# The front of a hybrid decoder layer: unrolled steps, raw x transposed early, its norm applied at the projection reads

## The chip, the cores and the metric

One NeuronCore of a Trainium2 chip runs the whole layer. The metric is the device time of one execution in microseconds (us). Smaller is better.

## The reference, cut to what matters

```python
u    = rms_norm(x, mix_norm_w)                       # x: 1024 tokens x 1024
proj = u @ w_in                                      # columns b, c, h (512 each), q (512), k and v (128 each)
y_conv = b * causal_dwconv3(c * h)                   # three taps over the tokens
q, k = rms_norm per head of 64
y_attn = sliding_window_attention(q, k, v, sinks)    # 8 heads on 2 key heads, blocks of 128, window 128, ALiBi
x = x + concat(rms_norm(y_conv), rms_norm(y_attn)) @ w_out
xn = rms_norm(x, ffn_norm_w)
x = x + moe_ffn(xn, ...)   # 64 experts, top 8 of them per token, and one shared expert
```

All of it is float32, but for a few small counting matmuls.

## The kernel before, in words

The kernel has two parts. The front works through the tokens in 8 tiles of 128 and does everything up to the router. The routed part then runs the shared expert and some 80 jobs of expert rows.

A semaphore orders every pair of instructions of different engines that depend on each other. Each engine's program is written out by hand and is run strictly in that order; a wait holds up all that is behind it on that engine. In the front each engine has a function `step`. Step T works on three tiles: N, the next one (its projections), T itself (its attention and its output projection), and B, the one before (its router).

PE runs in step T, in this order: `scores(T)`, `t_x(N)` (transposes of the normed x of the next tile), `project(N, 0)` and `project(N, 1)` (groups c and h), `t_xn(B)`, `t_p(T)`, `project(N, 2)` (b), `p_v(T)`, `router(B)`, `project(N, 3)` (q), `t_y(T)`, `project(N, 4)` (k and v), `position(B)`, `out_project(T, 0)`, `t_qk(N)`, `out_project(T, 1)`. A projection group of 512 columns is 8 matmuls of 128x128 by 512, each of which the trace shows as two instructions. `project` writes to two banks psP in turn, and ACT copies each out (`read_group`).

What lies around the first group: x has two tiles `x_sb`. The sum x1 of `x1_add(T)` (DVE, after `out_project(T, 1)`) goes to a tile of its own, and frees the x tile for SP's `load_x`. ACT squares the loaded x (`x_square`), DVE and POOL make the factor of the norm (`x_rms`, L476), ACT writes x times that factor to `xs` (`x_scale`, L909), PE transposes it, DVE reads the transposes into `uT` (`read_uT`, L1124), and `project(N, 0)` can start. The tile `xs` is also that of `xn`, the normed x1.

DVE in step T: `x_rms(N)`, `read_uT(N)`, `soft_a(T)`, `soft_b(T)` (scale, bias and maximum of the scores), `xn_make(B)`, `u_mul(N)` (c times h), `o_norm(T)`, `y_rms(T)`, `route(B)`, `read_yT(T)`, `read_pos(B)`, `qk_norm(N)`, `conv(N)`, `slots(B)`, `x1_add(T)`. The taps of the convolution need the product c*h moved by one and two tokens: SP stores it to DRAM and loads it twice, shifted (`shift_u`).

ACT in step T: `x_square(N)`, `x_scale(N)`, `exps(T)`, groups 0 and 1 of N, `read_xn(B)`, `read_p(T)`, group 2, `sigmoid(B)`, `y_square(T)`, `y_scale(T)` (both halves of y), groups 3 and 4, `read_qk(N)`, `x1_square(T)`.

POOL makes the reciprocal roots, stores xn and x1 to DRAM, and scatters the slots of an earlier tile: 8 indirect DMAs a tile (L538).

Of the kernel before, what the change touches and what calls it, by code (L numbers as in the profile page):

```python
# [16 lines left out]
ALU = mybir.AluOpType  # L17
# [3 lines left out]
P = 128  # L21
# [5 lines left out]
class Tile:  # L27


    def __init__(self, t, par, half):  # L30
        self.t, self.par, self.half = t, par, half

    def next(self):
        return Tile(self.t + 1, 1 - self.par, self.half + self.par)

    def prev(self):
        return Tile(self.t - 1, 1 - self.par, self.half - (1 - self.par))


def hymba_moe(nc, x, mix_norm_w, w_in, conv_w, q_norm_w, k_norm_w, sinks, conv_out_norm_w, attn_out_norm_w,  # L40
# [30 lines left out]
    with ExitStack() as ctx:  # L71
# [54 lines left out]
        x_sb = cut(2 * D).rearrange("p (b n) -> p b n", b=2)  # L126
        s_sb = cut(NH * 2 * P).rearrange("p (h k) -> p h k", h=NH)
        pT = cut(NH * 2 * P).rearrange("p (h k) -> p h k", k=P)
        xs = xn = cut(D)
        uT = cut(D).rearrange("p (k n) -> p k n", k=KT)  # L130
        yT = xnT = cut(D).rearrange("p (k n) -> p k n", k=KT)
        ys = x1 = cut(D)
        y_conv = cut(DC)
        y_attn = cut(DA)
# [93 lines left out]
        s_x1_st = sem("x1_st")  # L228
        s_x_rms = sem("x_rms")
        s_x_scaled = sem("x_scaled")  # L230
# [19 lines left out]
        s_y_sq = sem("y_sq")  # L250
        s_y_rms = sem("y_rms")
        s_y_scaled = sem("y_scaled")
# [36 lines left out]
        x_ld = [sem(f"x_ld{b}") for b in range(2)]  # L289
# [56 lines left out]
        def _(sp):  # L346
            def load_x(T):
                sp.dma_start(x_sb[:, T.par], x2[bass.ds(T.t * P, P), :]).then_inc(x_ld[T.par], 16)

            load_x(Tile(0, 0, 0))  # L350
# [5 lines left out]
            load_x(Tile(1, 1, 0))  # L356
            sp.dma_start(w_out_sb, w_out[0].rearrange("(k p) n -> p k n", p=P)).then_inc(s_wout_ld, 16)

# [7 lines left out]
            def shift_u(T):  # L366

                sp.wait_ge(s_u_ready, T.t + 1)
                sp.dma_start(u_dram[bass.ds(T.t * P + 2, P), :], u_sb).then_inc(s_u_st, 16)
                sp.wait_ge(s_u_st, (T.t + 1) * 16)  # L370
                carry(sp)
                sp.wait_ge(s_conv, T.t * 6)
                sp.dma_start(u1, u_dram[bass.ds(T.t * P + 1, P), :]).then_inc(s_u_ld, 16)
                sp.dma_start(u2, u_dram[bass.ds(T.t * P, P), :]).then_inc(s_u_ld, 16)

            shift_u(Tile(0, 0, 0))
            shift_u(Tile(1, 1, 0))
            sp.wait_ge(s_x1_ready, 1)
            load_x(Tile(2, 0, 1))
            with sp.Fori(0, (NT - 2) // 2 - 1) as i:  # L380
                for T in (Tile(2 * i + 1, 1, i), Tile(2 * i + 2, 0, i + 1)):
                    shift_u(T.next())
                    sp.wait_ge(s_x1_ready, T.t + 1)
                    load_x(Tile(T.t + 2, T.par, T.half + 1))
            for T in (Tile(NT - 3, 1, NT // 2 - 2), Tile(NT - 2, 0, NT // 2 - 1)):
                shift_u(T.next())
                if T.t == NT - 3:
                    sp.wait_ge(s_x1_ready, T.t + 1)
                    load_x(Tile(NT - 1, 1, NT // 2 - 1))


# [23 lines left out]
            sp.wait_ge(s_xn_st, 16 * (NT - 1))  # L415
            shared_rows(0, 0)
            shared_rows(1, 1)
            sp.wait_ge(s_xn_st, 16 * NT)
            sp.wait_ge(s_x1_st, 16 * NT)
# [41 lines left out]
        def _(pool):  # L461
# [19 lines left out]
            rsqrt_x(Tile(0, 0, 0))  # L481
# [34 lines left out]
            def store(T):  # L516

                pool.wait_ge(s_xn_ready, (T.t + 1) * 3)
                pool.dma_start(xn_dram[bass.ds(T.t * P, P), :], xn).then_inc(s_xn_st, 16)
                pool.dma_start(x1_dram[bass.ds(T.t * P, P), :], x1).then_inc(s_x1_st, 16)  # L520
# [4 lines left out]
            def rsqrt_y(T):  # L525
                rsqrt(st_y[:, 2, :], st_y[:, 1, :], 2, s_y_rms, T.t * 2 + 1)
# [15 lines left out]
            rsqrt_qk(Tile(0, 0, 0))  # L542
            for t in range(NT):
                if t + 1 < NT:
                    rsqrt_x(Tile(t + 1, 0, 0))
                if t >= 1:
                    rsqrt_xn(Tile(t - 1, 0, 0))
                    store(Tile(t - 1, 0, 0))
                if t >= 2:
                    scatter_slots(t - 2)  # L550
                rsqrt_y(Tile(t, 0, 0))
                if t + 1 < NT:
                    rsqrt_qk(Tile(t + 1, 0, 0))
            rsqrt_xn(Tile(NT - 1, 1, 0))
            store(Tile(NT - 1, 1, 0))
# [42 lines left out]
            pool.wait_ge(s_x1_st, 16 * NT)  # L598
# [27 lines left out]
        def _(pe):  # L626
# [3 lines left out]
            def t_x(T):  # L630

                pe.wait_ge(s_x_scaled, T.t + 1)
                for k in range(KT):
                    i = nc.tensor.transpose(psT[:, k, :], xs[:, k * P:(k + 1) * P], ident[:, :])  # L634
                i.then_inc(s_tx, 1)

            def project(T, g):

                _, c0, n = GROUPS[g]
                bank = (NGR * T.par + g) % 2  # L640
                if g == 0:
                    pe.wait_ge(s_uT_ready, T.t + 1)
                if not (isinstance(T.t, int) and T.t == 0 and g < 2):
                    pe.wait_ge(s_proj_out, T.t * NGR + (g - 1))
                for k in range(KT):
                    i = mm(psP[:, bank, 0:n], uT[:, k, :], w_in_sb[:, k, c0:c0 + n], k == 0, k == KT - 1)
                i.then_inc(s_proj, 1)

            def t_qk(T):
                pe.wait_ge(s_qk_norm, (T.t + 1) * 8)  # L650
                for hp in range(HP):
                    nc.tensor.transpose(psT[:, hp, :], qn[:, hp * P:(hp + 1) * P], ident[:, :])
                nc.tensor.transpose(psT[:, HP, :], kn[:, :], ident[:, :]).then_inc(s_tqk, 1)

            def scores(T, first):
# [3 lines left out]
                for kv in range(NKV):  # L659
                    r = slice(kv * HD, (kv + 1) * HD)  # L660
                    for hp in range(HP):
                        h = kv * HP + hp
                        o = psW[:, h // 2, (h % 2) * 2 * P:(h % 2 + 1) * 2 * P]
                        if not first:
                            mm(o[:, 0:P], qT[r, hp, :], kT[r, 1 - T.par, :], True, True)
                        i = mm(o[:, P:2 * P], qT[r, hp, :], kT[r, T.par, :], True, True)
# [21 lines left out]
            def t_y(T):  # L688
                pe.wait_ge(s_y_scaled, (T.t + 1) * 2)
# [24 lines left out]
            def position(T):  # L714

                pe.wait_ge(s_route, (T.t + 1) * N_RT)
                mm(psW[:, 1, 0:NE], ones_bf[:, :], msum[:, bass.ds(T.t, 1), :].rearrange("p a e -> p (a e)"),
                   True, False)
                mm(psW[:, 1, 0:NE], tri_bf[:, :], m_all[:, bass.ds(T.t, 1), :].rearrange("p a e -> p (a e)"),
                   False, False)  # L720
                mm(psW[:, 1, 0:NE], ones_bf[:, :], eo_bf[:, :], False, True).then_inc(s_position, 1)

            def step(T, first, last):
                N, B = T.next(), T.prev()
                scores(T, first)
# [787 lines left out]
```

## Time and profile before

| | |
|---|---|
| median of 3 runs | 1668.12 us (1663.58 to 1668.8) |
| the profiled execution | 1667.79 us, span 1666.0 us |
| PE busy | 1544.2 us, 93% of the span |
| DVE busy | 678.1 us, 41% |
| ACT busy | 302.4 us, 18% |
| POOL busy | 684.0 us, 41% |
| mean granted clock of TensorE | 0.945 |

PE (TensorE) has by far the most work. The granted clock of a stretch is a share of full speed: 1.00 is 2.4 GHz, 0.50 is 1.2 GHz. PE counts as busy for longer at the lower clock, so a busy share does not tell how much of the time is work at full speed.

### The profile page before, as it was taken

How to read it: one execution, taken by the hardware profiler on the slowest of the kernel's cores; microseconds unless marked ns; L12 is line 12 of the kernel's file. 1: busy time of each engine (PE TensorE's matmuls, PEld its weight loads, DVE VectorE, ACT ScalarE, POOL GpSimd, SP SyncE). 2: the span in 40 equal slices, each digit the busy share in tenths (PEclk: the TensorE clock that was granted, in tenths of full speed). 3: DMA queues.
4: the chain of work that ended last, by engine and by line, in shares of the span. 5: the costliest groups of instructions: out<-in, count | busy, mean ns of one | idle time of the engine just before them, and what ended most of it. 6: DMA issues, size and time to landing. Idle time of an engine off the chain costs nothing.

```text
span 1666.0 us, 24640 instructions
## 1 busy us (share of the span) xinstructions
PE 1544.2 (93%) x6767; PEld 704.6 (42%) x6768; DVE 678.1 (41%) x884; ACT 302.4 (18%) x573; POOL 684.0 (41%) x631
## 2 busy tenths in 40 slices
PE   7789899998997689999999999999999999999991
PEld 3455455555555445433333333333333333333330
DVE  1223442524425242434444444444444444444440
ACT  1223223232232100011111111111111111111110
POOL 2000212022021140045656566565666566565652
PEclk9799998898988789999999999999999999999995
DMA  9201101011116052388899988987889989888925
GB/s 353 77 26 45 38 19 57 13 44 41 28 45 252 26 152 88 124 296 297 270 317 287 348 266 281 314 245 234 263 275 340 348 274 327 274 271 265 301 31 114
DMA packets 72032, 319.36 MB, mean 192 GB/s; under 512 B 14935, under 2 KB 16472, under 8 KB 46532
## 3 DMA queue, kind: packets, MB, share of 16 engines
q1 hardware_dynamic: 41764, 237.52, 38.7%
q0 software_dynamic: 30240, 81.50, 20.3%
q8 instruction: 13, 0.21, 0.1%
q14 instruction: 15, 0.12, 0.0%
HBM read 280.11 MB, written 60.89 MB: 205 GB/s over the span
## 4 chain that ended last, share of the span: by engine, by line
PE 87%; DMA 4%; DVE 3%; issue 2%; POOL 1%; SPq 1%; ACT 1%; POOLq 0%; DVEq 0%; ACTq 0%
PE psP L628 50%; PE psW L628 27%; PE psT L765 5%; DMA area<-in_x_dram 1%; PE psW L795 1%; DMA u_dram<-zrow 1%; PE psW L674 1%; PE psT L634 1%; DMA out_dram<-area 1%; DVE area L1228 1%; DMA area<-xn_dram,gidx 1%; DVE area L1124 1%; ACT area L909 0%; SPq L352 0%; PE psT L705 0%
## 5 line engine op out<-in xcount | busy, mean ns | idle before, releaser
L628 PE MATMUL psP<-wts,area 128*64 (+2 forms) x1344 | 586.5, 592 | 14.4 <-DVE area L1124 11.8
L628 PE MATMUL psW<-wts,area 128*64 128x512 f32 (+2 forms) x1592 | 430.0, 596 | 4.9 <-DVE wts L1450 4.2
L628 PEld LDWEIGHTS psP<-wts,area 128*128 128x128 f32 (+1 forms) x1344 | 223.9, 171 | 326.9 <-issue 320.2
L628 PE MATMUL psP<-wts,bias 128*64 (+1 forms) x688 | 306.6, 598 | 1.3 <-DVE bias L1348 1.3
L628 PE MATMUL psP<-area 128*64 128x512 f32 x640 | 283.2, 595 | 0.0
L628 PE MATMUL psP<-area,bias 128*64 128x512 f32 x624 | 277.6, 598 | 0.0
L628 PEld LDWEIGHTS psW<-wts,area 128*64 128x64 f32 (+1 forms) x1592 | 150.8, 149 | 257.4 <-issue 256.4
L571 POOL COPY gidx<-area 128x1 int32 (+1 forms) x83 | 205.1, 2471 | 83.8 <-PE psT L765 58.1
L588 POOL DMA_INDIRECT out_dram<-area,sidx x79 | 119.3, 1510 | 261.6 <-ACT area L1049 160.8
L1442 DVE COPY area<-wts 128x4096 f32 x81 | 186.2, 2299 | 97.2 <-issue 88.1
L588 POOL DMA_INDIRECT x_dram<-area,sidx x79 | 167.7, 2123 | 24.4 <-issue 24.4
L628 PEld LDWEIGHTS psP<-wts,bias 128*64 128x64 f32 (+1 forms) x688 | 94.3, 142 | 177.6 <-issue 176.0
L1450 DVE COPY wts<-wts 128x2048 f32 x79 | 97.3, 1232 | 96.8 <-issue 95.6
L1033 ACT ACTIVATE kv_sb<-psP 128x256 f32<-128x256 f32 x87 | 33.4, 384 | 567.8 <-PE psP L628 567.8
L1049 ACT ACTIVATE area<-psW 128x1024 f32<-128x1024 f32 x79 | 81.0, 1026 | 256.3 <-PE psW L628 178.8
L574 POOL DMA_INDIRECT area<-xn_dram,gidx x83 | 92.0, 1108 | 76.6 <-POOL gidx L571 71.7
L1348 DVE COPY area<-psT 128x1024 f32<-128x1024 f32 x45 | 55.1, 1223 | 133.0 <-PE psT L765 124.4
L765 PEld LDWEIGHTS psT<-ident,area 128*128 128x128 f32 x712 | 78.4, 143 | 71.8 <-issue 71.8
L1348 DVE COPY bias<-psT 128x1024 f32<-128x1024 f32 x44 | 53.8, 1224 | 127.2 <-PE psT L765 127.2
L765 PE MATMUL psT<-ident,area 128*128 128x128 f32 x712 | 98.5, 282 | 3.9 <-DMA area<-xn_dram,gidx 3.9
L628 PEld LDWEIGHTS psP<-area 128*64 128x64 f32 x640 | 84.4, 137 | 0.0
L628 PEld LDWEIGHTS psP<-area,bias 128*64 128x64 f32 x624 | 82.6, 137 | 0.0
(206 smaller groups left out, 994.3 us busy)
## 6 DMA issues: line engine op xcount, KB each, us to landing
wts<-in_w_exp_gate_dram SPq DMA_DIRECT2D x64, 1024.0 KB
wts<-in_w_exp_up_dram SPq DMA_DIRECT2D x64, 1024.0 KB
wts<-in_w_exp_down_dram SPq DMA_DIRECT2D x64, 1024.0 KB
wts<-in_w_in_dram SPq DMA_DIRECT2D x4, 2048.0 KB, 17.6
area<-in_x_dram SPq DMA_DIRECT2D x8, 512.0 KB, 3.2
wts<-in_w_out_dram SPq DMA_DIRECT2D x1, 4096.0 KB, 18.3
area<-u_dram SPq DMA_DIRECT2D x16, 256.0 KB, 2.9
xn_dram<-area POOLq DMA_DIRECT2D x8, 512.0 KB, 3.0
```

The lines of the kernel that those rows point to most:

```text
L571: nc.gpsimd.tensor_copy(gidx[:, par:par + 1], tab_i[:, bass.ds(j - NSH, 1)]).then_inc(s_idx_cp, 1)
L574: pool.indirect_dma_start(out=xg[:, par], out_offset=None, in_=xn_dram[:, :], in_offset=bass.IndirectOffsetOnAxis(ap=gidx[:, par:par + 1], ...
L588: pool.indirect_dma_start(out=(out2, x1_dram)[b][:, :], out_offset=bass.IndirectOffsetOnAxis(ap=sidx[b][:, par:par + 1], axis=0), in_=ysb[ ...
L628: return nc.tensor.matmul(out_, lhsT, rhs, start=start, stop=stop)
L634: i = nc.tensor.transpose(psT[:, k, :], xs[:, k * P:(k + 1) * P], ident[:, :])
L674: i = nc.tensor.transpose(psW[:, n // 4, (n % 4) * P:(n % 4 + 1) * P], s_sb[:, h, half * P:(half + 1) * P], ident[:, :])
L765: i = nc.tensor.transpose(psT[:, k, :], xg[:, par, k * P:(k + 1) * P], ident[:, :])
L1033: A(sg, psP[:, par, 0:FE], ACT.Silu).then_inc(s_silu, 1)
L1049: A(ysb[:, par], psW[:, 2:4, :].rearrange("p a n -> p (a n)"), ACT.Copy).then_inc(s_y_ready, 1)
L1348: V.tensor_copy(xT[par], psT[:, :, :]).then_inc(s_xT_ready, 1)
L1442: V.tensor_copy(gu_b[par].rearrange("p m k f -> p m (k f)"), wts[:, bass.ds((e % NSLOT) * SLOTW, 2 * GUW)].rearrange("p (m n) -> p m n", m ...
L1450: V.tensor_copy(dn_b, wts[:, bass.ds((e % NSLOT) * SLOTW + 2 * GUW, FT * D)]).then_inc(s_dn_copy, 1)
```

## The change

The loop of the front is gone: the 8 steps are written out with constants. The order and the tiles change too:

- `t_x` transposes x as it was loaded, a step early: `t_x(NN)` for the tile after next stands between the two halves of `out_project(T)`, `read_uT(NN)` behind it on DVE. The factor of the norm is applied by ACT's `read_group` to all five groups. `x_scale` is gone.
- A step begins with `project(N, 0)`, then `scores(T)`, then `project(N, 1)`. The groups q and k, v are cut in pieces around `t_p`, `p_v` and `t_y`.
- `scores` takes the two key heads in turn (partitions 0 to 63, then 64 to 127), where it took all matmuls of one before those of the other.
- x has three tiles, and `x1_add` writes its sum in place over x. `load_x(NN)` waits until x1 of that buffer's last tile is stored to DRAM, and stands ahead of `shift_u(N)` on SP.
- `xn` has a tile of its own. `y_conv` and `y_attn` are scaled in place, each half with its own square, root and factor; those of `y_conv` come at the end of the step before. `conv(N)` stands before `o_norm(T)` on DVE; its last product (`conv_gate`) comes later.
- The transposes of q and k go to a bank of psW and to the free half of a psP bank.

```diff
-        def front(eng, step):
-
-            step(Tile(0, 0, 0), True, False)
-            with eng.Fori(0, (NT - 2) // 2) as i:
-                step(Tile(2 * i + 1, 1, i), False, False)
-                step(Tile(2 * i + 2, 0, i + 1), False, False)
-            step(Tile(NT - 1, 1, NT // 2 - 1), False, True)
+        def front(step):
+
+            for T in tiles:
+                N = tiles[T.t + 1] if T.t + 1 < NT else None
+                NN = tiles[T.t + 2] if T.t + 2 < NT else None
+                step(T, N, NN, tiles[T.t - 1] if T.t else None)
@@ SP @@
+            def step(T, N, NN, B):
+                if B and NN:
+                    sp.wait_ge(x1_st[B.par], (B.t // 2 + 1) * 16)
+                    sp.wait_ge(s_xn_ready, T.t * 3)
+                    load_x(NN)
+                if N:
+                    shift_u(N)
@@ PE @@
             def t_x(T):
 
-                pe.wait_ge(s_x_scaled, T.t + 1)
+                pe.wait_ge(x_ld[T.buf], T.use * 16)
@@ PE, scores @@
+                for hp in range(HP):
+                    for half in range(0 if T.t else 1, 2):
+                        for kv in range(NKV):
+                            r = slice(kv * HD, (kv + 1) * HD)
+                            h = kv * HP + hp
+                            o = psW[:, h // 2, ((h % 2) * 2 + half) * P:((h % 2) * 2 + half + 1) * P]
+                            i = mm(o, qT[r, hp, :], kT[r, T.par if half else 1 - T.par, :], True, True)
@@ PE @@
+            def step(T, N, NN, B):
+                first = B is None
+                if N:
+                    project(N, 0, range(0, 6 if first else KT))
+                if first:
+                    t_qk(T)
+                    project(N, 0, range(6, KT))
+                    pe.wait_ge(s_qkT, 2)
                     project(N, 1)
-                if not first:
+                scores(T)
+                if first:
+                    project(N, 2)
+                    project(N, 3, range(0, 3))
+                elif N:
+                    project(N, 1)
+                if B:
                     t_xn(B)
+                if B and N:
+                    project(N, 2)
                 t_p(T, first)
+                if B and N:
+                    project(N, 3, range(0, 3))
+                if first:
+                    project(N, 3, range(3, 5))
                 p_v(T, first)
+                if B:
                     router(B)
+                if N:
+                    project(N, 3, range(5 if first else 3, KT))
+                    project(N, 4, range(0, 4))
                 t_y(T)
+                if N:
+                    project(N, 4, range(4, KT))
...
                 out_project(T, 0)
+                if N:
                     t_qk(N)
+                if B:
+                    position(B)
+                if NN:
+                    t_x(NN)
                 out_project(T, 1)
@@ ACT, read_group @@
-                A(dst, psP[:, bank, 0:n], ACT.Copy).then_inc(s_proj_out, 1)
+                A(dst, psP[:, bank, 0:n], ACT.Copy, scale=st_x[:, 2:3]).then_inc(s_proj_out, 1)
@@ ACT @@
+            def step(T, N, NN, B):
+                first = B is None
+                if B:
+                    x1_square(B)
+                if N:
+                    read_group(N, 0)
+                if first:
+                    y_conv_square(T)
+                    y_conv_scale(T)
+                    read_group(N, 1)
                 exps(T, first)
+                if B and N:
                     read_group(N, 1)
+                if B:
                     read_xn(B)
+                if N:
+                    read_group(N, 2)
                 read_p(T, first)
+                y_attn_square(T)
+                if B:
                     sigmoid(B)
+                y_attn_scale(T)
+                if N:
                     read_group(N, 3)
                     read_group(N, 4)
+                if NN:
+                    x_square(NN)
+                if N:
+                    read_qk(N)
+                    y_conv_square(N)
+                    y_conv_scale(N)
@@ DVE @@
+            def step(T, N, NN, B):
+                first = B is None
+                if B:
+                    x1_add(B)
+                    xn_make(B)
                 soft_a(T, first)
                 soft_b(T, first)
+                if N:
                     u_mul(N)
+                    conv(N)
                 o_norm(T)
+                y_attn_rms(T)
+                if B:
                     route(B)
                 read_yT(T)
+                if N:
+                    qk_norm(N)
+                if NN:
+                    x_rms(NN)
+                if B:
                     read_pos(B)
+                if NN:
+                    read_uT(NN)
+                if N:
+                    conv_gate(N)
+                if B:
                     slots(B)
+                if N:
+                    y_conv_rms(N)
@@ DVE, ahead of the steps @@
+            x_rms(tiles[0])
             dve.wait_ge(s_mixw_ld, 16)
+            read_uT(tiles[0])
             constants()
+            u_mul(tiles[0])
+            read_uT(tiles[1])
+            qk_norm(tiles[0])
+            x_rms(tiles[1])
+            conv(tiles[0])
+            conv_gate(tiles[0])
+            y_conv_rms(tiles[0])
```

PE does `t_x(tiles[1])` right behind the projections of tile 0, and SP loads x of tile 2 right behind `w_out`. ACT's order ahead of the steps is `x_square` of tile 0, its five groups, `x_square` of tile 1, `read_qk` of tile 0.

## Rows read from the trace of the kernel before

**Rows 1.** Chain that ended last, one step of the front: start, us, what.
```profile
249.39 1.24 DVE area L1228
250.78 3.12 DMA area<-in_x_dram
...
256.01 1.16 ACT area L909
257.22 1.98 PE psT L634 x8
259.33 1.24 DVE area L1124
...
260.69 16.53 PE psP L628 x32
277.22 0.87 PE psT L705 x8
278.10 1.75 PE psW L674 x16
279.84 6.87 PE psP L628 x16
286.71 5.30 PE psW L628 x48
...
299.81 3.46 PE psP L628 x16
...
317.76 1.24 DVE area L1228
```

**Rows 2.** Windows: stretch, its us, busy us (instructions) by engine, clock, DMA.
```profile
252.00:256.00 4.00, 3.88 (x23) 3.58 (x21) 0.15 (x1) 2.33 (x3) 0.56 (x1) 0.52 0.29 116
...
272.00:276.00 4.00, 4.00 (x11) 1.81 (x10) 0.00 (x0) 0.00 (x0) 3.08 (x4) 1.00 0.18 58
```

**Rows 3.** Timeline of PE, the scores of one step at full clock.
```profile
183.10 3.47 PE L628 MATMUL psW<-kT,qT 64*128 64x128 f32 x32 [1.41 <-DVE area L1228]
```

**Rows 4.** Chain that ended last, gate and up of a routed job.
```profile
802.21 7.02 PE psP L628 x32
```

**Rows 5.** Timeline of ACT in the same step.
```profile
265.58 0.51 ACT L944 ACTIVATE area<-area,st_s 128x256 f32<-128x256 f32 x1 [8.42 <-DVE st_s L1198]
...
269.53 0.19 ACT L946 ACTIVATE st_s<-st_s 128x8 f32<-128x8 f32 x1
...
287.37 1.28 ACT L989 ACT_TABLE_LOAD   x1
```

**Rows 6.** Timeline of POOL in the same step, first store and last scatter.
```profile
268.62 0.65 POOL L519 DMA_DIRECT2D xn_dram<-area  x1 [2.37 <-DVE area L1237]
...
279.72 0.96 POOL L538 DMA_INDIRECT slot_table<-pay,slot_i  x1 [0.30 <-issue]
```

**Rows 7.** Timeline of SP's queue in the same step.
```profile
278.79 0.36 SPq L369 DMA_DIRECT2D u_dram<-area  x1
287.92 0.33 SPq L373 DMA_DIRECT2D area<-u_dram  x1
```

**Rows 8.** Timeline of DVE in the same step: the router's first and last operation.
```profile
293.60 0.22 DVE L1254 TENSOR_TENSOR bi<-sc,rbias 128x64 f32<-128x64 f32 x1
...
298.71 0.26 DVE L1283 TENSOR_SCALAR w_all<-mb,wsum 128x64 f32 x1
```

**Rows 9.** Chain that ended last, ahead of and at the end of step 0.
```profile
32.12 15.71 DMA u_dram<-zrow
...
114.37 1.24 DVE area L1228
```

**Rows 10.** Timeline of PE, the five groups of tile 0.
```profile
11.09 33.92 PE L628 MATMUL psP<-wts,area 128*128 128x512 f32 x80 [1.49 <-DVE area L1124]
```

**Rows 11.** Timeline of DVE: last product of tile 0's convolution.
```profile
56.88 0.69 DVE L1148 TENSOR_TENSOR area<-area 128x512 f32<-128x512 f32 x1
```

**Rows 12.** Timeline of DVE: the sum x1 of tile 6, before the last step.
```profile
522.56 1.23 DVE L1228 TENSOR_TENSOR area<-psW,area 128x1024 f32<-128x1024 f32 x1 [2.06 <-PE psW L628]
```

More of the change, by code:

```diff
@@ L27, with __init__ @@
 class Tile:
[L30 to L37, printed above, removed]
+    def __init__(self, t):
+        self.t, self.par, self.buf, self.use = t, t % 2, (t + 1) % 3, t // 3 + 1
+        self.rows = slice(t * P, (t + 1) * P)
 def hymba_moe(nc, x, mix_norm_w, w_in, conv_w, q_norm_w, k_norm_w, sinks, conv_out_norm_w, attn_out_norm_w,
@@ L368, in shift_u @@
                 sp.wait_ge(s_u_ready, T.t + 1)
-                sp.dma_start(u_dram[bass.ds(T.t * P + 2, P), :], u_sb).then_inc(s_u_st, 16)
+                sp.dma_start(u_dram[T.t * P + 2:(T.t + 1) * P + 2, :], u_sb).then_inc(s_u_st, 16)
                 sp.wait_ge(s_u_st, (T.t + 1) * 16)
[L371 to L389, printed above, removed]
+                if T.t:
+                    sp.wait_ge(s_conv, T.t * 6)
+                sp.dma_start(u1, u_dram[T.t * P + 1:(T.t + 1) * P + 1, :]).then_inc(s_u_ld, 16)
+                sp.dma_start(u2, u_dram[T.t * P:(T.t + 1) * P, :]).then_inc(s_u_ld, 16)
+            shift_u(tiles[0])
+            def step(T, N, NN, B):
[5 more added lines that the diff above has]
+                    shift_u(N)
+            front(step)
             def load_gu(slot, gate, up):
@@ L540, in scatter_slots @@
                                             in_=pay[:, t, j, :], in_offset=None).then_inc(s_sc_tab, 16)
[L542 to L555, printed above, removed]
+            rsqrt_qk(tiles[0])
+            rsqrt_x(tiles[1])
+            rsqrt_yc(tiles[0])
+            def step(T, N, NN, B):
+                if B:
+                    rsqrt_xn(B)
+                    store(B)
+                if T.t >= 2:
+                    scatter_slots(T.t - 2)
+                rsqrt_ya(T)
+                if N:
+                    rsqrt_qk(N)
+                if NN:
+                    rsqrt_x(NN)
+                if N:
+                    rsqrt_yc(N)
+            front(step)
+            rsqrt_xn(tiles[-1])
+            store(tiles[-1])
             scatter_slots(NT - 2)
@@ L721, in position @@
                 mm(psW[:, 1, 0:NE], ones_bf[:, :], eo_bf[:, :], False, True).then_inc(s_position, 1)
-            def step(T, first, last):
-                N, B = T.next(), T.prev()
-                scores(T, first)
-                if not last:
-                    pe.wait_ge(s_qkT, (T.t + 1) * 2)
-                    t_x(N)
-                    project(N, 0)
-                    project(N, 1)
-                if not first:
-                    if not last:
-                        pe.wait_ge(s_uT_ready, N.t + 1)
+            def step(T, N, NN, B):
[6 more added lines that the diff above has]
+                    pe.wait_ge(s_qkT, 2)
+                    project(N, 1)
+                scores(T)
[5 more added lines that the diff above has]
+                if B:
@@ L821, in _ @@
             pe.wait_ge(s_const_pool, 3)
-            T0 = Tile(0, 0, 0)
-            t_x(T0)
+            t_x(tiles[0])
             for g in range(NGR):
                 pe.wait_ge(win_ld[g], 16)
-                project(T0, g)
-            t_qk(T0)
+                project(tiles[0], g)
+            t_x(tiles[1])
             pe.wait_ge(s_const_ld, 16 * N_CONST)
-            front(pe, step)
-            TL = Tile(NT - 1, 1, NT // 2 - 1)
+            front(step)
+            TL = tiles[-1]
             t_xn(TL)
@@ L1308, in slots, with step @@
                                 ALU.add).then_inc(s_slots, 1)
-            def step(T, first, last):
-                N, B = T.next(), T.prev()
-                if not last:
-                    x_rms(N)
-                if not last:
-                    read_uT(N)
+            def step(T, N, NN, B):
+                first = B is None
+                if B:
+                    x1_add(B)
+                    xn_make(B)
                 soft_a(T, first)
                 soft_b(T, first)
-                if not first:
-                    xn_make(B)
-                if not last:
+                if N:
@@ L1358, in h_mul @@
                                        op0=ALU.mult, op1=ALU.mult).then_inc(s_h_ready, 1)
-            front(dve, step)
-            TL = Tile(NT - 1, 1, NT // 2 - 1)
+            front(step)
+            TL = tiles[-1]
+            x1_add(TL)
             xn_make(TL)
```

267 lines of the change are left out of this document (116 added, 151 removed).

## The prediction

> **What bounds the kernel now.** I read the windows first: PE has by far the most busy time, so the question is where PE is not working at full speed. The routed part is dense. There, gate and up of one job follow the other jobs' work without a gap [rows 4], and this change does not touch it. The front is another matter, and the chain that ended last shows why. Each step of the front has one place where the chain leaves PE: from the sum x1 through a DMA of x, ACT, transposes and DVE, and back to PE's first projection [rows 1]. The reader is to see that the chain goes x1 at 249.39, x loaded from 250.78, scaled at 256.01, transposed at 257.22, read at 259.33, projected at 260.69. PE has only the scores of the step to put into these 11.30 us.
>
> What is lost there. Scores take 3.47 us at full clock [rows 3] and eight transposes 0.87 us (the same kind as the eight at 277.22) [rows 1], 4.34 us of useful work in 11.30 us, so 6.96 us are idle or slow. Then the clock: around the scores the windows show it granted at 0.52, later in the step at 1.00 [rows 2]; these are the levels of 1.2 and 2.4 GHz, and PE had been waiting before it fell. The two projection groups behind the gap take 16.53 us, against 6.87 us for one group later in the step [rows 1]: 16.53 - 2 x 6.87 = 2.79 us. Together 9.75 us are lost in a step of 317.76 - 249.39 = 68.37 us, and 58.62 us are PE's work at full clock.
>
> **The change, part by part: the steady step.** With x transposed before the second half of the output projection, `read_uT(NN)` (1.24 us) lies under the 6.9 us of that half, and `project(N, 0)` can follow at once. The loads of x have a whole step. The square of x and the root lie on ACT and DVE beside PE's work, and the factor is only needed when group 0 is read. `x_scale` falls away from ACT, where it cost 1.16 us; the factor in `read_group` is a scale operand of a copy that ran anyway, so I cost it at nothing (it lies under the next group's 6.87 us). The same holds for the new squares and roots of the half y_conv. What the earlier order exposes is then the length of PE's own work, if nothing new is late. I walk through a step from its start (0, the end of `out_project`), with the durations of [rows 1, 5, 8].
>
> `project(N, 0)` to 6.9, under which x1 is added, squared, normed: about 5.7. Scores, then `project(N, 1)`, `t_xn` 0.87, `project(N, 2)`, `t_p` 1.75, three eighths of group 3 (2.58), `p_v` (two thirds of the 5.30 us, as 32 of the 48 instructions: 3.53). Behind the scores stand scale, maximum and exponentials: `soft_a` and `soft_b` followed `read_uT` (to 260.57) on DVE and the first exponential came at 265.58, 5.0 us later, and the nine take 269.72 - 265.58 = 4.14 us [rows 1, 5]. That is 9.1 us, under the 14.6 us of two groups and `t_xn`. It does hold up ACT's read of group 1, so the product u comes about 10.6 us behind the scores.
>
> Scores alternate over the two halves of partitions. The nearest row for two halves worked in turn is that of a routed job, where 32 instructions of 512 columns, on two halves of the output columns, take 7.02 us [rows 4], while one group of 16 takes 6.87 us [rows 1]: pairs run at the same time. By that row the scores take 1.74 us. The nearest row for small matmuls whose weight load is as long as the matmul is `p_v`: it streams half the columns of the scores and takes 5.30 / 48 = 0.110 us for each instruction, just what the scores take (3.47 / 32 = 0.108). So there the pace is that of loading 128 columns of weights, and if these loads do not overlap for two halves, the scores stay at 3.47. I take the middle, 2.60 us, as each row is near in one respect: 0.87 us gained a step, both ends (0 and 1.73) kept.
>
> The Trainium skill (TensorEngine Tiling (Array Packing), Key Properties) says that different tiles can execute weight loads and matmuls in parallel. By it the scores would take 1.74 us. No trace before shows this for halves of the partitions; it is a rival below.
>
> Where a wait takes a new place. On DVE `conv(N)` now stands before `o_norm(T)`, so DVE is held by the round trip of u through DRAM, and behind it wait `o_norm`, the root of y, `route(B)` and `read_yT`, and for the last PE's output projection. SP's store of u took until 287.92 from 278.79, 9.13 us [rows 7], as POOL's scatters ran until 280.68 [rows 6]; it landed 7.2 us behind the last of them. In the new step the scatters follow the xn store, which comes at 6.0, and end at 6.0 + (280.68 - 268.62) = 18.1. The scores end at 9.5, u is stored from 20.3, lands by 18.1 + 7.2 = 25.3 at the latest, the loads (as x's 3.1 us) by 28.7, and five operations of 0.7 us [rows 11] end at 32.4. `p_v` ends at 6.87 + 2.6 + 6.87 + 0.87 + 6.87 + 1.75 + 2.58 + 3.53 = 31.9. So DVE is late by 0.5 us at most, and not at all when the store lands sooner. If that cover is gone, every us of a later landing is a us of DVE.
>
> The second narrow place: counted from the end of `p_v`, PE has the router 1.77, five eighths of group 3 4.29, half of group 4 1.73, `t_y` 0.87, the rest 1.73: 10.4. ACT and DVE have `o_norm` and the square (to about 2.0), the table load that now stands between square and sigmoid (1.28 [rows 5]; before it lay ahead of a wait), the sigmoid, to 3.6, then the router's chain 298.97 - 293.60 = 5.37 [rows 8] and `read_yT` 1.24: 10.3. They are level. I take 0.3 us of stall a step for the two places; the bounds are 0 and 1.5. POOL's queue has only roots behind the scatters, needed at 33; SP's `load_x(NN)` waits for the x1 store at about 10 and holds `shift_u`, which is needed at 20.
>
> Period: 58.62 - 0.87 + 0.3 = 58.05 us. The six steps from 114.37 [rows 9] to 522.56 [rows 12] take 408.19 us now, and would take 348.3: 59.9 us less.
>
> **Step 0.** Before, tile 1 waited for tile 0's convolution, because its `x_rms` stood behind it on DVE. That ended at 57.57 [rows 11], as SP stood until 47.83 for the table's first filling [rows 9]. PE had been done with tile 0 at 45.01 [rows 10]. Now `t_x(1)` follows at once. The first projection starts about 0.7 us sooner (no scaling, w_in just there), so tile 0 ends at 44.3, uT of tile 1 is there at 46.5, groups 0 and 1 with `t_qk` between end at 61.0, eight scores at 62, group 2 at 69.5. One more load of x in SP's queue (512 KB) delays the filling by some 1.4 us, so tile 0's convolution ends at 59; ACT reads group 0 behind it, which group 2 needs (at 62). The rest is PE's row: 3 eighths of group 3 2.6, `t_p` 0.9, 2 eighths 1.7, `p_v` 1.8, 3 eighths 2.6, half of group 4 1.7, `t_y` 0.9, half 1.7, `out_project` 6.9, `t_qk` and `t_x` 1.4, `out_project` 6.9, together 29.1: x1 at 98.7 instead of 114.37, 15.7 us less. Uncertain by 4 us either way, mostly by what the convolution delays.
>
> **The last step** has no projections to cover anything, so its chain stays. Two operations of ACT (square and scale of y_conv, about 0.7 us each) leave it, and the softmax starts a little sooner: 2 us less, bounds 0 and 3. The weights of the routed part wait for the last projection as before.
>
> **Sum.** 59.9 + 15.7 + 2 = 77.6 us. The profiled execution took 1667.79 us, 0.3 us under the median, so no correction: 1667.8 - 77.6 = 1590 us.
>
> **Rivals.**
>
> *The scores overlap in full.* For it: the routed pairs. Against: the pace of `p_v`. Six steps by another 0.87 us, less some of it for the DMA round trip, which does not move with them: about 5 us, 1585 us. The sentence of the Trainium skill on tiles (TensorEngine Tiling (Array Packing), Key Properties) speaks for this one.
>
> *The table switch costs more than its instruction.* Now on the narrow path, ahead of the sigmoid. Before, it stood ahead of a long wait, so what it costs beyond 1.28 us cannot be seen; if it is as much again, the router's chain is late by 1.1 us in each of six steps: 1597 us. Against it: nothing that the rows show. The Trainium skill (ScalarE: Activation LUTs, What ACT_TABLE_LOAD costs) gives a drain of about 1.38 us on top of 1.28, which speaks for this rival; no row here shows it.
>
> *A wait takes the place of the old one.* DVE stays blocked in `conv(N)`, because the store of u lands later than now. For it: the store is issued only 2 us behind the scatters. At 2.5 us more a step: 1605 us.
>
> *Most of the gain is lost*, because several engines' orders bind at once, and half of the 9.75 us remains: about 1625 us.
>
> *Slower than before.* One mechanism: the same wait of DVE on u. To eat 77.6 us it must cost 12.9 us more in each of the six steps, that is a store landing over 22 us after its issue, where the slow ones took 9.1. The scatters would have to be that much later in the queue: `slots(B)` before them comes near the end of a step. From 13 us late on this decides, and a result of 1672 us would be 13.6 us late.
>
> **How the numbers follow.** Chances: forecast (1587 to 1594) 0.42; full overlap 0.21; table switch 0.15; wait on DVE 0.13; most lost 0.05, slower 0.02, and 0.02 for a gain above all this (under 1581), for step 0 is only bounded. The range 1581 to 1608 holds the first four less the tail of the fourth. A measurement tells changes of over 0.3% (5 us): faster 0.97, same 0.01, slower 0.02.
>
> **What would show it.** In the profile after: no chain piece of a DMA of x or of `x_scale` in the front; clock 1.00 from step 1 to step 6; x1 sums 58 us apart, the first at 99; scores of 1.7 to 3.5 us; small PE waits at most, for `read_yT` or for pT. Wrong would be: sums over 60 us apart with PE waiting for DVE, a clock that still falls in the steps, or a start later than 103.

## The result and the profile after

The changed kernel takes 1606.84 us (median of 4 runs, 1599.65 to 1609.03), the kernel before 1667.3 us in the same set of runs. The ratio is 0.9633, 95% interval 0.9617 to 0.9649: faster by 60 us. The forecast was 1590, with a range of 1581 to 1608: direction and range held, but 17 us of the forecast gain are missing, and the result lies only 1.2 us inside the upper end of the range, near the rival "a wait takes the place of the old one" (1605 us, chance 0.13) and not in the band of the forecast itself (1587 to 1594, chance 0.42). The place of the missing time can be read off the sums x1, one at the end of each step. These are rows of DVE's timeline after (start, us, line and operation):

```profile
98.71 1.23 DVE L1256 TENSOR_TENSOR area<-psW,area 128x1024 f32<-128x1024 f32 x1 [4.10 <-PE psW L634]
...
155.94 1.22 DVE L1256 TENSOR_TENSOR area<-psW,area 128x1024 f32<-128x1024 f32 x1 [2.60 <-PE psW L634]
...
409.52 1.23 DVE L1256 TENSOR_TENSOR area<-psW,area 128x1024 f32<-128x1024 f32 x1 [2.60 <-PE psW L634]
```

The first sum comes at 98.71 (forecast 98.7; before 114.37 [rows 9]). Step 1 takes 57.23 us. Steps 2 to 5 take 253.58 us, 63.4 us each, where 58.05 were forecast. Step 6 ends at 465.93, 56.41 us later. The profiled execution's span is 1607.2 us. From that last sum to the end of the span it has 1141.3 us; before it was 1666.0 - 522.56 = 1143.4 us [rows 12].

So two steps run as PE alone would have it, and the four between do not. These are signs that the prediction had named for being wrong: sums over 60 us apart with PE waiting for DVE, and a clock that still falls in the steps. The chain of waits that ended last, in step 2 of the changed kernel (start, us, what):

```profile
174.67 0.70 DVE area L1150
175.39 10.69 DMA u_dram<-area
186.10 0.32 SPq L371
186.46 2.94 DMA area<-u_dram
189.43 0.69 DVE area L1157
...
193.26 0.70 DVE area L1239
194.01 0.51 issue
194.72 0.88 ACT L1005
195.60 0.42 issue
196.01 0.23 ACT sc L1005
196.27 0.24 DVE bi L1284
...
201.18 1.23 DVE area L1251
202.45 10.17 PE psW L634 x16
```

The chain of before stepped from the sum to a load of x [rows 1]. That is gone. In its place the chain goes through the store of u (L1150 is the product), the two shifted loads, the convolution, `o_norm` (L1239), the table load and the sigmoid, the router, `read_yT` (L1251), and only then PE. And the first half of the output projection takes 10.17 us, not 6.87. The windows of the same step (stretch, its length, busy us and instructions of PE, of PE's weight loads, DVE, ACT and POOL, then clock, DMA share and GB/s) show why:

```profile
194.00:198.00 4.00, 2.32 (x15) 1.84 (x15) 1.64 (x14) 3.40 (x6) 0.57 (x1) 1.00 0.00 0
198.00:202.00 4.00, 1.74 (x9) 1.18 (x7) 3.40 (x15) 1.51 (x3) 0.00 (x0) 0.97 0.01 2
202.00:206.00 4.00, 3.55 (x4) 1.52 (x5) 2.43 (x6) 0.00 (x0) 1.34 (x1) 0.50 0.02 4
```

PE had waited twice when the granted clock fell to 0.50, the level of 1.2 GHz. The delay is paid twice: 4.4 us of idle time (1.68 us ahead of `t_y`, 2.71 us ahead of the output projection), and 3.3 us of slow matmuls behind it, 7.7 of the 65.13 - 57.24 = 7.9 us by which step 2 is longer than an undisturbed one (57.24 us: e2 below).

Why does the store of u land so late? SP's queue in steps 2 and 6, from its timeline (L345 is the load of x, L367 the store of u, L371 waits for it):

```profile
165.94 0.33 SPq L345 DMA_DIRECT2D area<-in_x_dram  x1
175.39 0.32 SPq L367 DMA_DIRECT2D u_dram<-area  x1
186.10 0.32 SPq L371 DMA_DIRECT2D area<-u_dram  x1
...
429.01 0.32 SPq L367 DMA_DIRECT2D u_dram<-area  x1
434.75 0.32 SPq L371 DMA_DIRECT2D area<-u_dram  x1
```

Step 6 has no tile left to load and lands the store in 5.7 us; steps 2 to 5 load x and need 10.7, 8.5, 9.2 and 11.4 us. Step 1 loads x without scatters beside it, and needs 2.0 us. These are landings of one execution of one kernel; the experiments show how far they spread. The DMA view of step 2 has the scatters at 11.0 us from issue to landing, that of step 6 at 5.8 us (kind, count, median us):

```profile
slot_table<-pay,slot_i POOLq DMA_INDIRECT x8, 11.0
```

```profile
slot_table<-pay,slot_i POOLq DMA_INDIRECT x8, 5.8
```

POOL's timeline has the last scatter of step 2, then of step 6. The store lands 13.2 us behind its end in the one and 8.2 us in the other; before it was 7.2 us [rows 6, 7].

```profile
171.92 0.95 POOL L536 DMA_INDIRECT slot_table<-pay,slot_i  x1 [0.30 <-issue]
...
425.56 0.95 POOL L536 DMA_INDIRECT slot_table<-pay,slot_i  x1 [0.31 <-issue]
```

Two more points, on the scores and on the table load, are in the timelines of PE and ACT in step 2. The scores take 2.06 us, against 3.47 [rows 3]; the chain, which counts up to the next instruction, has 2.01. The table load begins where the square ends, and the sigmoid where the table load ends:

```profile
162.70 2.06 PE L634 MATMUL psW<-kT,qT 64*128 64x128 f32 x32
```

```profile
194.52 0.19 ACT L987 ACTIVATION_READ_ACCUMULATOR junk<-area 128x1 f32 x1
194.72 1.28 ACT L1005 ACT_TABLE_LOAD   x1
196.01 0.22 ACT L1005 ACTIVATE sc<-psW 128x64 f32<-128x64 f32 x1
```

### The profile page after: what moved, and what is told of

The parts are those of the page before. It is cut to its first block, busy times and chain, and to the rows that moved or that the text cites. A ratio compares the mean times of both kernels' runs of the same rounds, so it can differ in the third digit from the quotient of the medians.

```text
span 1607.2 us, 24184 instructions
## 1 busy us (share of the span) xinstructions
PE 1509.5 (94%) x6767; PEld 677.5 (42%) x6768; DVE 678.7 (42%) x892; ACT 294.3 (18%) x564; POOL 686.8 (43%) x639
## 3 DMA queue, kind: packets, MB, share of 16 engines
q0 software_dynamic: 30240, 81.50, 21.4%
## 4 chain that ended last, share of the span: by engine, by line
PE 83%; DMA 6%; DVE 5%; ACT 2%; issue 1%; POOL 0%; SPq 0%; POOLq 0%; DVEq 0%; ACTq 0%
PE psP L634 46%; PE psW L634 29%; PE psT L787 6%; DMA u_dram<-area 2%; ACT area L960 1%; PE psW L817 1%; DMA wts<-in_w_in_dram 1%; DMA area<-u_dram 1%; DVE area L1211 1%; DVE st_s L1221 1%; DMA out_dram<-area 1%; DMA area<-xn_dram,gidx 1%; PE psW L685 1%; PE psT L642 0%; DVE area L1251 0%
## 5 line engine op out<-in xcount | busy, mean ns | idle before, releaser
L634 PE MATMUL psP<-wts,area 128*64 (+2 forms) x1344 | 571.1, 577 | 9.1 <-DMA wts<-in_w_in_dram 5.3
L634 PE MATMUL psW<-wts,area 128*64 128x512 f32 (+2 forms) x1592 | 440.5, 604 | 17.9 <-DVE area L1251 14.1
L634 PEld LDWEIGHTS psP<-wts,area 128*128 128x128 f32 (+1 forms) x1344 | 216.2, 166 | 308.1 <-issue 297.9
L634 PEld LDWEIGHTS psW<-wts,area 128*64 128x64 f32 (+1 forms) x1592 | 154.7, 151 | 278.0 <-issue 261.7
L471 POOL TENSOR_TENSOR st_y<-st_y,minus_half 128x1 f32<-128x1 f32 x16 | 8.9, 556 | 220.0 <-DVE st_y L1105 220.0
```

The lines of the kernel that those rows point to most:

```text
L634: return nc.tensor.matmul(out_, lhsT, rhs, start=start, stop=stop)
```

## The experiments

Ten kernels were run, in three sets. Ratios are to the kernel before, in the same set. Periods are distances between sums x1 in the profiled executions.

**e1, the load of x behind the store of u.** From the changed kernel:

```diff
             def step(T, N, NN, B):
+                if N:
+                    shift_u(N)
                 if B and NN:
                     sp.wait_ge(x1_st[B.par], (B.t // 2 + 1) * 16)
                     sp.wait_ge(s_xn_ready, T.t * 3)
                     load_x(NN)
-                if N:
-                    shift_u(N)
```

> The change kept, but SP stores and loads u of tile N first and loads x of the tile after next behind that. Theory A (the load of x runs into the scatters of the slots, both crawl, and the store of u is queued behind them: it landed 8.4 to 11.4 us after its issue in steps 2 to 5, 5.7 us in step 6, which has scatters and no load of x): the store lands in about 5.7 us in steps 2 to 5, the periods fall from 61.6 to 65.1 us to about 57 us, in all some 20 us less, 1587 us. Theory B (the scatters alone delay the store): landing stays 8 to 11 us, the time stays within 5 us of 1607.

1584.46 us, ratio 0.9516 (0.9499 to 0.9534). Periods 57.94, 57.24, 57.24 and 58.31 us in steps 2 to 5. The store of u, in SP's timeline of step 2:

```profile
176.59 0.32 SPq L367 DMA_DIRECT2D u_dram<-area  x1
182.13 0.32 SPq L371 DMA_DIRECT2D area<-u_dram  x1
...
183.03 0.38 SPq L345 DMA_DIRECT2D area<-in_x_dram  x1
```

It lands in 5.5 us (4.2, 4.4 and 5.7 in the next steps). Theory A's outcome came: with the load of x behind the store, the landings are 4 to 6 us shorter than the changed kernel's, and almost all of the lost time is back. Steps 2 and 5, which landed last, still have 0.7 and 1.1 us of it. The profiled execution is the fastest of the four (1581.51 us), and e7 below shows that the size of the effect on the landing is not fixed.

**e2, the convolution later on DVE.**

```diff
                 if N:
                     u_mul(N)
-                    conv(N)
                 o_norm(T)
...
                 if NN:
                     x_rms(NN)
+                if N:
+                    conv(N)
                 if B:
                     read_pos(B)
```

> The change kept, but the five operations of the convolution stand on DVE behind the norm of q and k and the root of x, as they did before the change, and not ahead of o_norm. Both theories on the DMA (A: load of x; B: scatters) agree that the store of u lands as late as now, 8 to 11 us; if DVE's place for the convolution is what turns this into a wait of PE, periods fall to about 57 us and the time to about 1586 us. Rival: the convolution then makes the end of the step late on DVE (3.6 us more ahead of the read of uT, slots and the root of y_conv), and the periods stay over 60 us.

1581.93 us, ratio 0.9497 (0.9481 to 0.9513), the fastest kernel of this study. Every period of steps 1 to 5 is 57.24 us, step 6 has 56.42. PE waits for nothing in these steps. The store of u still lands late (8.5, 6.4, 5.8 and 8.6 us in steps 2 to 5, 2 to 3 us sooner than in the changed kernel), and it no longer matters. SP's timeline of step 2:

```profile
176.83 0.32 SPq L367 DMA_DIRECT2D u_dram<-area  x1
185.31 0.32 SPq L371 DMA_DIRECT2D area<-u_dram  x1
```

So the slow DMA is one half of the cause, and the place of the waiting instruction on DVE the other. Mending the second removes the wait in every step, mending the first nearly so. The rival, that the convolution would then make the end of the step late, did not come.

**e3, the scatters later on POOL.**

```diff
-                if T.t >= 2:
-                    scatter_slots(T.t - 2)
                 rsqrt_ya(T)
+                if T.t >= 2:
+                    scatter_slots(T.t - 2)
```

> The change kept, but POOL starts the scatters of the slots behind the root for y_attn, some 28 us later in the step, so that neither the load of x nor the store of u meets them. Theory A and B both: the store of u lands in about 2.1 us as in step 1, the convolution ends well before p_v does, periods about 57 us, 1586 us. Rival (the store is slow for another reason, such as the stores of xn and x1): landing stays over 5 us. A risk is the root for q and k, which then stands behind 10 us of scatters on POOL: if it is late, PE waits at the transposes of q and k, 1 to 3 us a step.

1586.97 us, ratio 0.9526 (0.951 to 0.9542). The store of u lands in 2.0 to 2.5 us in every step, with the load of x still ahead of it: without scatters beside it, that load does no harm. The foreseen side effect is there: PE waits in steps 2 to 6 for `kn`, behind POOL's root, 2.2 us in all. Three periods are 58.65 us and step 6 is 57.76, each 1.3 to 1.4 us over e2's. In step 6 the wait for `kn` is 1.06 us; in the three it is under 0.4, and another of 0.6 us stands ahead of the output projection, whose cause the trace does not name.

```profile
PE psW L662 <- DVE kn L1201: 2.2, 4, 1.1
```

**e7, e1 and e2 together.**

> e1 and e2 together: the load of x behind the store of u on SP, and the convolution behind the norm of q and k on DVE. Theory (both mend the same wait): the time of e2, 1582 us within 2 us, with the store of u landing in 3 to 6 us. Rival (each mends a part of its own): 5 us or more below e2.

1583.91 us, ratio 0.9494 (0.9474 to 0.9514), the same as e2 within both intervals. In its profiled execution all steps 1 to 5 have 57.24 us. Both mend the same wait. One part of the expectation missed: the store of u did not land in 3 to 6 us but in 6.9, 6.8, 6.0 and 7.4. SP's timeline of step 2:

```profile
176.41 0.32 SPq L367 DMA_DIRECT2D u_dram<-area  x1
183.35 0.32 SPq L371 DMA_DIRECT2D area<-u_dram  x1
```

SP and POOL work in the order of e1 here, which landed in 4.2 to 5.7 us, and e2, with the load of x ahead of the store, is barely later in the mean (7.3 us against 6.8). So what the load of x costs the store among scatters is 5 us between the changed kernel and e1, and 0.5 us between e2 and e7. No run says what makes this difference.

**e4, the scores in the old order.**

```diff
-                for hp in range(HP):
-                    for half in range(0 if T.t else 1, 2):
-                        for kv in range(NKV):
+                for kv in range(NKV):
+                    for hp in range(HP):
+                        for half in range(0 if T.t else 1, 2):
```

> The change kept, but the scores take all heads of one key head first, as before the change. Theory (halves of the partitions taken in turn run at the same time): 32 instructions take 3.47 us again where they take 2.0, so 1.5 us more in steps 1 to 7 where PE sets the pace, less where DVE waits for the store of u, which does not move with the scores: 3 to 10 us more in all, 1610 to 1617 us. Rival (the shorter scores came from the clock alone): 2.0 us stay.

1599.93 us, ratio 0.9607 (0.9591 to 0.9623). The expectation missed: it was to be slower than the changed kernel and is a little faster. The two ratios, from different sets of runs, lie close (their intervals overlap). The profiled steps 1 to 6 take 361.0 us together against 367.2, but that compares the fastest execution of e4 with the slowest of the changed kernel. Its steps without a wait (1 and 3) are 58.68 us, 1.44 us longer. In the others `p_v` ends 1.4 us later, so DVE is less late; and u, stored 1.7 us later, landed sooner after that (8.0, 5.2, 6.9 and 8.5 us). That the later store is what made it land sooner is not shown: e9 stores u at the same point of the step and needs 10.0, 7.1, 8.0 and 9.5 us. The chain of step 3 shows scores of 3.43 us and no wait, with an output projection at full clock:

```profile
225.83 3.43 PE psW L634 x32
...
262.36 6.87 PE psW L634 x16
```

**e9, the old order of the scores on top of e2.** The edit is that of e4.

> On top of e2_conv_late, the scores of one key head first, then the other's, as before the change. With DVE's wait gone PE sets the pace, so the price of the order of the scores shows undisturbed: 3.47 - 2.0 = 1.45 us in each of steps 1 to 6, half of it in step 0, a little in step 7: 9 to 10 us more than e2, 1591 us. That e4 was faster than the changed kernel would then come from the wait alone. Rival (alternation costs PE something elsewhere, which e4 saved): e9 is no slower than e2.

1593.67 us, ratio 0.9557 (0.9535 to 0.958), against 0.9497 for e2 in another set. Periods 58.68 us in steps 1 to 5, 1.44 us over e2's. The timelines of PE give the scores, first e9, then e2:

```profile
223.59 3.50 PE L634 MATMUL psW<-kT,qT 64*128 64x128 f32 x32
```

```profile
220.42 2.06 PE L634 MATMUL psW<-kT,qT 64*128 64x128 f32 x32
```

The alternation is worth 1.44 us a step where PE sets the pace. It costs PE nothing elsewhere, so what e4 gained on the changed kernel must lie in the wait.

**e5, the transposes of x back at the start of the step, on top of e2.**

```diff
@@ PE @@
-                if NN:
-                    t_x(NN)
                 out_project(T, 1)
...
+                if B and N:
+                    t_x(N)
                 if N:
                     project(N, 0, range(0, 6 if first else KT))
@@ DVE @@
+                if B and N:
+                    read_uT(N)
                 if B:
                     x1_add(B)
...
-                if NN:
-                    read_uT(NN)
```

> On top of e2_conv_late (whose steps take 57.24 us), the early transposition undone: PE transposes raw x of tile N at the start of step T (steps 1 to 6) and waits for DVE to read the transposes before the first projection. Theory: per step only the reading of the transposes and its two hand-overs are exposed, about 1.24 + 0.2 = 1.5 us, and the clock does not fall over so short a gap: 6 x 1.5 = 9 us more than e2, 1591 us. Rival: the clock falls too, 3 us more a step, 1609 us.

1593.82 us, ratio 0.9556 (0.9533 to 0.958). Periods 58.87 us, 1.63 over e2. PE's timeline has the gap, and the group behind it at full clock (7.13 us; in e2 the same group takes 7.03):

```profile
217.91 7.13 PE L634 MATMUL psP<-wts,area 128*128 128x512 f32 x16 [1.32 <-DVE area L1145]
```

**e6, load and transposes of x back behind the sum, the norm still at the projection reads, on top of e2.**

```diff
@@ SP @@
-            load_x(tiles[2])
...
-                if B and NN:
-                    sp.wait_ge(x1_st[B.par], (B.t // 2 + 1) * 16)
-                    sp.wait_ge(s_xn_ready, T.t * 3)
-                    load_x(NN)
+                if B and N:
+                    if T.t >= 2:
+                        sp.wait_ge(x1_st[T.par], ((T.t - 2) // 2 + 1) * 16)
+                        sp.wait_ge(s_xn_ready, (T.t - 1) * 3)
+                    sp.wait_ge(s_x1_ready, T.t)
+                    load_x(N)
@@ PE @@
+                if B:
+                    scores(T)
+                if B and N:
+                    t_x(N)
                 if N:
                     project(N, 0, range(0, 6 if first else KT))
...
-                scores(T)
+                if first:
+                    scores(T)
...
-                if NN:
-                    t_x(NN)
```

The square of x moves behind `x1_square(B)` on ACT, `x_rms` and `read_uT` behind `xn_make(B)` on DVE, the root behind `store(B)` on POOL.

> On top of e2_conv_late, load and transposition of x put back to where they were before the change (x of tile N loaded only when x1 of the tile before is summed; scores, then transposes, then the first projection, in steps 1 to 6), but the norm still applied as the projections are read. Theory: the chain x1, load 3.1 us, transposes 1 to 2 us, reading 1.24 us is exposed again without square, root and scaling: the first projection starts some 8.3 us after the sum instead of 11.3, and the clock still falls. Periods about 65 us instead of 57.2 and 68.0: 6 x 8 = 47 us more than e2, 1629 us. Rival: without a fall of the clock (the gaps are shorter) periods of 62 us, 1610 us.

1621.49 us, ratio 0.9731 (0.9704 to 0.9757). Six periods of 62.9 us in the mean, between the two expectations: 61.5 to 61.8 in steps 2 to 4, 63.2 in step 1 and 64.9 and 64.5 in steps 5 and 6. The chain of step 3:

```profile
223.07 1.24 DVE area L1261
...
224.38 3.04 DMA area<-in_x_dram
...
228.77 1.24 DVE area L1150
...
230.05 14.00 PE psP L635 x32
```

The first projection starts 6.98 us behind the sum, 8.3 was expected, and the clock does not fall (14.00 us for two groups, 16.53 before [rows 1]), though PE waits 1.36, 1.02 and 1.49 us around the scores and the transposes. Where x landed later (in step 5 PE waited 2.82 us ahead of the transposes, against 1.02 in step 3), the windows have the clock at 0.84 and 0.73 behind it:

```profile
352.00:356.00 4.00, 2.13 (x10) 1.38 (x11) 2.40 (x3) 1.15 (x2) 2.57 (x5) 0.84 0.66 262
356.00:360.00 4.00, 4.00 (x8) 1.75 (x7) 3.80 (x5) 0.00 (x0) 3.09 (x4) 0.73 0.02 1
```

**b1, the kernel before, its front written out, nothing else.**

```diff
-            with eng.Fori(0, (NT - 2) // 2) as i:
+            for i in range((NT - 2) // 2):
```

> The kernel before with nothing but its front written out: the loops of the front on all engines, SP's too, replaced by eight steps with constants, in the old order. Theory: no time, within 4 us of before, as step 0 and step 7 were already written out and PE's waits in the loop are all for x. Rival (loop and register instructions cost something each step): 5 to 12 us less.

1667.7 us, ratio 0.9998 (0.9986 to 1.0011). Writing out is worth nothing by itself.

**b2, the kernel before, the key heads in turn, nothing else.** The loops of the scores are those of the changed kernel.

> The kernel before with nothing but the order of the scores changed: both key heads in turn. Theory: the scores take 2 instead of 3.5 us at full clock, but they lie in a gap that the load of x ends, so nothing is gained; within 3 us of before in the steps 1 to 6, and the clock may fall a little sooner, as PE is idle longer: up to 6 us slower. Rival: the shorter scores count in full, 9 us less.

1664.91 us, ratio 0.9986 (0.9974 to 0.9999), 2 us less. PE's timeline in step 4: the scores are down to 2.06 us (5.28 in the same step of before, at the lower clock), and PE waits 4.66 us ahead of the transposes where it waited 1.10; they take 1.97 us as before.

```profile
320.96 2.06 PE L628 MATMUL psW<-kT,qT 64*128 64x128 f32 x32 [1.41 <-DVE area L1227]
327.67 1.97 PE L634 MATMUL psT<-ident,area 128*128 128x128 f32 x8 [4.66 <-ACT area L908]
```

## Why the prediction was right, and where its sum was off

*The bound.* Right. PE's own work at full clock was put at 58.62 us a step with the scores of old; e9, whose PE never waits in these steps and which has the old scores, has 58.68.

*The load chain leaves the path.* Right, and now split: of the 68.0 us of a step before, putting everything back but norm and scaling (e6) leaves 62.9, the late transposes alone (e5) cost 1.63 over e2's 57.24. Over steps 1 to 6 e2 has 57.1 in the mean, so the early load and the early transposition together are worth 5.8 us a step. The difference of 5.1 us between before and e6 holds the norm outside the chain, the faster scores, fewer falls of the clock and the other changes of order that e6 keeps; no run here parts it further.

*The scores.* The middle of two bounds was taken, 2.60 us, and 2.01 measured: the rival with full overlap was nearly right (1.74). `p_v`'s pace, which spoke against it, does not hold for alternating halves: b2, which changes only the order, has 2.06 us too, and PE's weight-load rows cover the 32 loads in 1.86 us against 3.30 before, of 188 ns each in the mean both times. That it is the loads of the two halves that overlap is read from these rows, not shown by a run of its own. What the Trainium skill says of tiles in parallel (TensorEngine Tiling (Array Packing), Key Properties) agrees with them. The sum lost 0.59 us a step by it, on the slow side.

*The table switch.* This rival fell. From the end of the square to the start of the sigmoid there are 1.30 us, of which the load is 1.28; the drain of 1.38 us that the Trainium skill adds (ScalarE: Activation LUTs, What ACT_TABLE_LOAD costs) does not show here.

*The wait on DVE.* This is the step that was off: "u is stored from 20.3, lands by 18.1 + 7.2 = 25.3 at the latest", and so a stall of 0.3 us with a bound of 1.5. The store was issued at 19.5 us into step 2 and landed at 30.2. The 7.2 us came from one step, and "at the latest" was more than the trace before allowed: in step 2 of the kernel before the store landed 8.4 us behind the last scatter. The last scatter there, in POOL's timeline, and the end of the store, in SP's:

```profile
210.60 0.96 POOL L538 DMA_INDIRECT slot_table<-pay,slot_i  x1 [0.31 <-issue]
```

```profile
219.92 0.34 SPq L373 DMA_DIRECT2D area<-u_dram  x1
```

The 7.2 us also came from a kernel in which no load of x stood among the scatters; in the changed kernel it was 1 us short without one (step 6), and 4 to 7 us with one. The change puts the load there, and I had cleared `load_x(NN)` only for holding up SP, not for what it does to the DMA queues. The mechanism was named as a rival (2.5 us a step, 1605 us); what it had too small was the size, 24.6 us over four steps, for the clock falls behind each wait, and the rival had no term for that: one output projection a step took 8.8 or 10.2 us where 6.87 is full clock, 9.2 us of the 24.6. e2 shows the link through DVE and e3 that through the scatters; e1 shows that the load of x matters, with its size open (e7). That the range held is owed to this rival, which lay at its upper end.

*The second narrow place.* No stall came of it: from `o_norm` to the end of `read_yT` the chain needs 202.41 - 193.26 = 9.15 us in step 2, where 10.3 was put against PE's 10.4, and in e2 PE waits for nothing.

*Step 0 and the last step.* 98.71 measured for 98.7, and its parts fit as well: tile 0's groups end at 44.7 (44.3 forecast), the scores of tile 0 start at 61.4 (61.0). No run here takes this gain of 15.7 us, a quarter of the whole, apart; the other kernels with the changed front have their first sum at 98.1 to 100.0. The last stretch is 2.1 us shorter for 2, and that is luck in part: this stretch takes 1134.8 to 1148.6 us in the profiled executions of the kernels with the changed front.

The terms again, each step against the 58.05 us forecast: steps 2 to 5 took 253.58 - 232.20 = 21.4 us more, step 1 0.8 less (scores, no stall), step 6 1.6 less (also no transposes of x). That is 18.9 us, and with the 1590.2 us of the forecast and 0.1 less in the last stretch the 1609.03 us of the profiled execution.

*The slower rival* needed 12.9 us a step in six, and the wait cost 6.2 us in each of four. It named the right mechanism, far too large.

## What to carry to other kernels

When a transfer is moved, ask what it meets in the DMA queues at its new time, not only what it holds up in its issuer's program: here the next store landed in 8.5 to 11.4 us with a load of 512 KB ahead of it among eight tiny scatters, and in 4.2 to 5.7 us with that load moved behind it (e1), though a second pair of kernels (e2, e7) shows only 0.5 us. An instruction that waits for a round trip through DRAM belongs as late on its engine as its own consumer allows, for all behind it inherits the wait: e2's one move was enough, however late the store. And a small wait of PE is to be priced with the slow matmuls behind it: here 4.4 us of waiting cost 7.7.

## What the runs showed of the hardware

- Eight scatters of 128 rows of 8 bytes delay a store far out of proportion to their size. A store of 256 KB landed in 2.0 us where no scatters preceded it (step 1 of every kernel with the changed front), in 2.5 to 7.4 us behind eight scatters (e1, e7, and step 6 of the changed kernel, e2, e4, e5 and e9), and in 5.2 to 11.4 us where a load of 512 KB stood among them (steps 2 to 5 of the changed kernel, e2, e4, e5 and e9). The ranges overlap, and the same order of SP and POOL gave 4.2 to 5.7 us in one profiled execution (e1) and 6.0 to 7.4 in another (e7). The load is not needed for a slow store: before the change one issued ahead of the last scatter took 9.13 us [rows 6, 7]. What in the queues makes it so was not taken apart.
- Two halves of the partitions (64 rows each) worked in turn take 2.01 us for 32 instructions that take 3.47 us one half after the other.
- A wait of 1.32 us between dense stretches left the clock at 1.00 (e5), and so did waits of 1.36, 1.02 and 1.49 us in one step of e6. Waits of 1.68 and 2.71 us in step 2 of the changed kernel were followed by 0.50.
- A longer PE stage can cost nothing where another wait binds: e4 adds 1.44 us a step and is no slower than the changed kernel. Where that wait is mended (e9 against e2) the same stage costs its full length.
